# Differential attention of a hybrid diffusion step: scores by half partitions, two sets of score banks, work moved between engines

## The reference

```
def diff_attention(q, k, v, lam):
    # q (B,Lq,H,2,dh), k (B,Lk,H,2,dh), v (B,Lk,H,2dh); blocks of 128 queries
    s = einsum('bqhmd,bkhmd->bhmqk', qblk, k) * dh ** -0.5
    p = softmax(s, axis=-1)
    a = p[:, :, 0] - lam * p[:, :, 1]
    return einsum('bhqk,bkhe->bqhe', a, v)
...
o_d = diff_attention(q_d, k_all, v_all, lam)
o_d = rmsnorm(o_d, diff_subln_g) * (1.0 - lam_init)
branch_d = o_d.reshape(B, L, DIFF_V_W) @ w_diff_out
```

## Time and profile before

| what | value |
|---|---|
| time of the runs | 1432.61, 1429.55, 1432.03 us, median 1432.03 |
| the profiled execution, first to last instruction | 1432.7 us |
| TensorE busy | 1363.0 us, 95% |
| VectorE, ScalarE, GpSimd busy | 638.5, 452.0, 112.9 us |
| attention, from the first scores to the last stored output tile | 651.30 to 796.99 us |

### The profile page before, as it was taken

How to read it: one execution, slowest core, us unless ns; L and a number is a source line. 1 busy time by engine, 2 the same in 40 slices (tenths; PEclk the granted TensorE clock), 3 DMA queues, 4 the chain that set the end, 5 groups by cost and what they waited for, 6 DMA issues and landing times.

```text
span 1432.7 us, 24335 instructions
## 1 busy us (share of the span) xinstructions
PE 1363.0 (95%) x9545; PEld 1291.3 (90%) x9545; DVE 638.5 (45%) x935; ACT 452.0 (32%) x777; POOL 112.9 (8%) x205
## 2 busy tenths in 40 slices
PE   4899999999999999998999899989999999999996
PEld 1699998899999999996777599989999999999996
DVE  3733112466557534645777644352324232333244
ACT  5421313344211122216777522242211122212223
POOL 1011000300111111202111300000000000000000
PEclk9999999999999999999999999999999999999998
DMA  9444231143444343530000014202121212221211
GB/s 303 146 116 118 59 88 44 53 134 116 144 150 137 103 128 101 168 128 30 0 0 0 30 59 147 89 30 88 59 88 61 87 59 88 73 75 61 72 45 73
DMA packets 100820, 127.05 MB, mean 89 GB/s; under 512 B 3433, under 2 KB 91986, under 8 KB 100770
## 3 DMA queue, kind: packets, MB, share of 16 engines
q1 hardware_dynamic: 90624, 95.20, 21.1%
q0 software_dynamic: 8928, 30.09, 6.7%
q10 hardware_dynamic: 1218, 1.07, 0.2%
HBM read 115.34 MB, written 4.72 MB: 84 GB/s over the span
## 4 chain that ended last, share of the span: by engine, by line
PE 88%; DVE 4%; issue 2%; SPq 2%; ACT 2%; POOL 1%; DMA 1%; DVEq 0%; ACTq 0%; POOLq 0%
PE psum L340 49%; PE psum L355 26%; PE psum L760 4%; PE psum L787 2%; PE psum L774 2%; SPq L481 1%; PE psum L321 1%; DVE probs L1359 1%; PE psum L762 1%; PE psum L671 1%; DMA ada_a<-in_w_ada 1%; POOL diag L635 1%; PE psum L388 1%; PE psum L389 1%; PE psum L722 1%
## 5 line engine op out<-in xcount | busy, mean ns | idle before, releaser
L305 DVE TENSOR_TENSOR w_lo<-w_raw,w_hi 128x2048 fp32r<-128x2048 f32 x78 | 178.7, 2291 | 307.8 <-ACT w_hi L300 299.8
L340 PE MATMUL psum<-h_hi,w_lo 128*128 128x320 f32 x1344 | 308.5, 311 | 3.4 <-DVE hf L431 1.4
L340 PE MATMUL psum<-h_hi,w_hi 128*128 128x320 f32 x1344 | 307.4, 310 | 0.0
L340 PE MATMUL psum<-h_lo,w_hi 128*128 128x320 f32 x1344 | 307.2, 310 | 0.0
L340 PEld LDWEIGHTS psum<-h_hi,w_lo 128*128 128x128 f32 x1344 | 225.4, 189 | 4.4 <-issue 4.3
L340 PEld LDWEIGHTS psum<-h_lo,w_hi 128*128 128x128 f32 x1344 | 225.9, 189 | 0.0
L340 PEld LDWEIGHTS psum<-h_hi,w_hi 128*128 128x128 f32 x1344 | 225.7, 189 | 0.0
L300 ACT ACTIVATE w_hi<-w_raw 128x2048 fp32r<-128x2048 f32 x77 | 146.8, 1906 | 149.1 <-PE psum L355 97.7
L355 PE MATMUL psum<-w_lo,h_hi 128*128 128x256 f32 x480 | 136.1, 283 | 0.0
L355 PE MATMUL psum<-w_hi,h_lo 128*128 128x256 f32 x480 | 135.8, 283 | 0.0
L355 PE MATMUL psum<-w_hi,h_hi 128*128 128x256 f32 x480 | 135.8, 283 | 0.0
(11 more groups left out here) (214 smaller groups left out, 1842.6 us busy)
## 6 DMA issues: line engine op xcount, KB each, us to landing
w_raw<-in_w_in SPq DMA_DIRECT2D x32, 1024.0 KB, 5.9
ada_b<-in_w_ada POOLq DMA_DIRECT2D x32, 512.0 KB, 4.1
w_raw<-in_w_ffn_gate SPq DMA_DIRECT2D x11, 1024.0 KB, 5.1
w_raw<-in_w_ffn_up SPq DMA_DIRECT2D x11, 1024.0 KB, 5.1
ada_a<-in_w_ada SPq DMA_DIRECT2D x8, 1024.0 KB, 12.4
w_raw<-in_w_ffn_down SPq DMA_DIRECT2D x8, 1024.0 KB, 5.1
w_raw<-in_w_ret_out SPq DMA_DIRECT2D x4, 1024.0 KB, 5.1
swapped<-qk_d POOLq DMA_DIRECT2D x32, 128.0 KB, 2.5
```

Of the source, the lines that this page charges most:

```text
L305: dve.tensor_tensor(w_lo[s][:, :, :], w_raw[s][:, :, :], w_hi[s][:, :, :].bitcast(F32), ALU.subtract).then_inc(w_lo_done, 1)
L340: last = pe.matmul(bank(4 * par + 2 * j + h, HALF), w[:, k, cs], x[:, k, h * HALF:(h + 1) * HALF], start=(k == 0 and n == 0), stop=(k == K ...
```

## The change

- The scores of map m are computed from the 64 partitions that hold it, for queries and keys alike, by matmuls over 64 partitions. `qz` and its copies and the clearing of `qz` on GpSimd are gone. A latent tile takes five matmuls: keys of 128, 384, 512, 128 and 128, in turn from the lower and the upper half, with a wait (`at_shared`) ahead of the fifth, which shares a bank with the first.
- There are two sets of three score banks (0 to 2 and 3 to 5); tile n uses set n % 2 and waits for the exponentials of tile n - 2. The two maps lie 896 columns apart, so that one maximum instruction (line 1303 of the new kernel) reads both.
- The maps are combined on GpSimd in two instructions, a product in place (line 624) and a sum (line 626).
- The transposes go to banks 6 and 7: four blocks in bank 6, the fifth in the first quarter of bank 7. The outputs go to the third quarter of bank 7, for all tiles. The fifth transpose of tile n therefore waits until the output of tile n - 1 has been read (`at_oe`).
- The output is read by VectorE, not ScalarE: a scaled copy (line 1318) and then a product with a row sum (line 1320) that waits for the copy.
- All 40 tiles are written out with no loop. Slot s holds on TensorE `outputs(s-4)`, `weights_T(s-3)`, `scores(s+1)`; on VectorE `evacuate_o(s-4)`, `factor(s-1)`, `maximum(s+1)`; on ScalarE `evacuate_T(s-3)`, `exp(s)`.

```diff
             def scores(n):
+                if n >= 2:
+                    pe.wait_ge(at_e, 2 * n - 2)
...
+                    pe.matmul(bank(b0 + 1, P), qk_d[m0, h, q], kc_T[m0, h, :], start=True, stop=True).then_inc(at_shared, 1)
+                    pe.matmul(bank(b0 + 2, LAT - P), qk_d[m1, h, q], qk_d[m1, k, P:LAT], start=True, stop=True)
+                    pe.matmul(bank(b0), qk_d[m0, h, q], qk_d[m0, k, 0:LAT], start=True, stop=True)
+                    pe.matmul(bank(b0 + 2, P, LAT - P), qk_d[m1, h, q], kc_T[m1, h, :], start=True, stop=True)
+                    pe.wait_ge(at_shared, n - h + 1)
+                    last = pe.matmul(bank(b0 + 1, P, LAT - P), qk_d[m1, h, q], qk_d[m1, k, 0:P], start=True, stop=True)
...
+            def weights_T(n):
                 pe.wait_ge(at_a, n + 1)
+                if n >= 1:
                     pe.wait_ge(at_aT, n)
+                for c in range(keys_of(n) // P):
+                    if c == LAT_TILES and n >= 1:
+                        pe.wait_ge(at_oe, n)
+                    last = pe.transpose(bank(6 + c // 4, P, (c % 4) * P), probs[:, n % 3, 0, c * P:(c + 1) * P], ident[:, :])
...
+            for slot in range(-1, QT + 4):
+                if 0 <= slot - 4:
+                    outputs(slot - 4)
+                if 0 <= slot - 3 < QT:
+                    weights_T(slot - 3)
+                if slot + 1 < QT:
+                    scores(slot + 1)
...
+            def maximum(n):
+                dve.wait_ge(at_s, n + 1)
+                at_, apart = 3 * (n % 2) * BANK, (896 if n % TILES < LAT_TILES else 2 * BANK)
+                both = psum[:, at_:at_ + 2 * apart].rearrange("p (m k) -> p m k", m=2)[:, :, 0:keys_of(n)]
+                dve.reduce_max(sm[:, n % 8, 0:2], both, axis=AX.X, negate=True).then_inc(at_max, 1)
...
+            def evacuate_o(n):
+                h, t = n // TILES, n % TILES
+                x, r0, out = bank(7, P, 2 * P), sm[:, n % 8, 4:5], o_nat[:, t, h * P:(h + 1) * P]
+                if t == LAT_TILES:
+                    dve.wait_ge(k_stored, 16)
+                dve.wait_ge(at_o, n + 1)
+                dve.tensor_scalar(out, x, r0, None, ALU.mult).then_inc(at_oc, 1)
+                dve.wait_ge(at_oc, n + 1)
+                dve.scalar_tensor_tensor(junk_o[:, :], x, r0, out, ALU.mult, ALU.mult,
+                                         accum_out=stats[:, n:n + 1]).then_inc(at_oe, 1)
...
+            for slot in range(-1, QT + 4):
+                if 0 <= slot - 4:
+                    evacuate_o(slot - 4)
+                if 0 <= slot - 1 < QT:
+                    factor(slot - 1)
+                if slot + 1 < QT:
+                    maximum(slot + 1)
```

More of the change, by code:

```diff
@@ L766, in scores @@
                 last.then_inc(at_s, 1)
-            def weights_T(h0, t0, first=False):
-                h, t, n = tile_of(h0, t0)
+            def weights_T(n):
                 pe.wait_ge(at_a, n + 1)
-                if not first:
+                if n >= 1:
                     pe.wait_ge(at_aT, n)
-                for c in range(TILES if t < LAT_TILES else 1):
-                    last = pe.transpose(bank(4 + c // 4, P, (c % 4) * P), probs[:, PBUF[t], 0, c * P:(c + 1) * P], ident[:, :])
+                for c in range(keys_of(n) // P):
+                    if c == LAT_TILES and n >= 1:
+                        pe.wait_ge(at_oe, n)
+                    last = pe.transpose(bank(6 + c // 4, P, (c % 4) * P), probs[:, n % 3, 0, c * P:(c + 1) * P], ident[:, :])
@@ L815, in _ @@
-            pe.wait_ge(at_oe, 2 + DH * TILES)
+                if n >= 1:
+                    pe.wait_ge(at_oe, n)
+                hs = slice(h * P, (h + 1) * P)
+                chunks = keys_of(n) // P
+                for c in range(chunks):
+                    val = v_d[:, LAT_TILES, hs] if t == LAT_TILES else v_d[:, c, hs] if c < LAT_TILES else v_cache[:, hs]
+                    last = pe.matmul(bank(7, P, 2 * P), aT[:, n % 3, c, :], val, start=(c == 0), stop=(c == chunks - 1))
+                last.then_inc(at_o, 1)
@@ L1075, in _ @@
+            set_table(ACT.Exp)
+            for slot in range(QT + 3):
+                if slot >= 3:
+                    evacuate_T(slot - 3)
+                if slot < QT:
+                    exp(slot)
+                if slot == QT:
+                    set_table(ACT.Sqrt)
             root("normo", DH * TILES)
@@ L1361, in _ @@
-            maximum(0, 0, 0)
-            maximum(0, 0, 1)
-            maximum(0, 1, 0)
-            weights(0, 0, 0)
-            maximum(0, 1, 1)
-            weights(0, 0, 1)
-            maximum(0, 2, 0)
-            weights(0, 1, 0)
-            maximum(0, 2, 1)
-            weights(0, 1, 1)
-            with dve.Fori(0, DH - 1) as h:
-                for t in range(2, TILES + 2):
-                    maximum(h, t + 1, 0)
-                    weights(h, t, 0)
-                    maximum(h, t + 1, 1)
-                    weights(h, t, 1)
@@ L1377, in _ @@
-            for t in range(2, TILES):
-                if t + 1 < TILES:
-                    maximum(DH - 1, t + 1, 0)
-                weights(DH - 1, t, 0)
-                if t + 1 < TILES:
-                    maximum(DH - 1, t + 1, 1)
-                weights(DH - 1, t, 1)
-            dve.wait_ge(at_oe, 2 + DH * TILES)
+            def maximum(n):
[3 more added lines that the diff above has]
+                dve.reduce_max(sm[:, n % 8, 0:2], both, axis=AX.X, negate=True).then_inc(at_max, 1)
```

184 lines of the change are left out of this document (54 added, 130 removed).

## The result

| | before | changed |
|---|---|---|
| median, us | 1432.03 (5 runs, 1429.08 to 1433.95) | 1443.76 (5 runs, 1440.39 to 1447.4) |
| profiled span, us | 1432.7 | 1442.1 |

The changed kernel takes 1.0067 times as long (95% interval 1.0045 to 1.009): 6 to 13 us more. The forecast was 1439 us, slower.

A forecast was written before the change was run, and what follows sets the result against it. TensorE, all but full in the attention stage, was taken to bound the kernel. Heads of 18.0 us and a longer stage end shift the last transpose by 6.5 us: 1432.7 + 6.5 = 1439.2, stated as 1439, range 1428 to 1464.

The forecast's parts named there:

- The ring of a latent slot: Per latent tile: maximum, output read, signal, fifth transpose, scores, signal, next maximum form one chain of 3.94 us.
- The other slots: Slots of a head around the prompt tile, from maximum 2 to 3, 3 to 4, 4 to 0: 2.9, 2.94, 4.27 us.
- Halves side by side: Latent tile's scores on TensorE: lower and upper array halves overlap in part, 1.2 us from first to last start.
- my two ends: Bounds on a latent tile's scores, first to last start: 2.03 us without overlap, 0.96 with full overlap.
- The drain at each change of row set: Rival: TensorE's array empties twice a slot, 0.34 us per latent slot, 9.5 us in all, 1448 to 1449; chance 0.15.
- my lower end: Latent tile's scores with the array halves fully overlapping: 0.96 us from first to last start.
- my bounds: GpSimd's product when combining the maps: between 0.8 and 1.6 us.
- The clock: Rival: TensorE's clock falls because it idles; a head some 23.5 us, the time about 1478; chance 0.04.
- Both ends: Attention stage: first maximum near 653.9, tile 4's at 663.0; last transpose 11.4 us behind the last maximum, 3.27 a tile.
- The sum: Last transpose at 800.4 against 793.93 us, a shift of 6.5 that goes to the kernel's end: 1439 us.
- the first rival: Array halves do not run side by side in the scores: latent slots 4.77, a head 20.9, 1461 us; chance 0.25.

The follow-up runs named there:

- the control: Kernel before, without the zero-padded GpSimd copies and with TensorE's loop written out, each score matmul over all 128 partitions (output not the reference's): 1429.93 us, ratio 0.9972.
- scores first: Changed kernel with TensorE taking the scores of tile s+1 ahead of the transposes of tile s-3: 1469.32 us, ratio 1.026.
- exponentials first: Changed kernel with scores ahead of transposes on TensorE, and exponentials ahead of the copy of the transposed weights on ScalarE: 1536.32 us, ratio 1.0691.
- one bank set: Changed kernel with all tiles using score banks 0 to 2, a tile's scores waiting for the previous tile's exponentials: 1567.68 us, ratio 1.0921.
- the version with the short end: Kernel with ScalarE's output copy, plus two late sets of transposes in free score banks ahead of outputs and tile 38 combined on VectorE: 1421.28 us, ratio 0.9908.

## Why the prediction was right, step by step

- *The ring of a latent slot.* Right in place, and nearly in size: 3.87 and 3.88 us measured, 3.94 forecast. Term by term: maximum 1.41 (1.42), output read and signal 0.79 (0.90), fifth transpose to scores 0.26 (0.11), scores 1.09 (1.20), signal 0.33 (0.31). The ring was shown by taking one instruction out of it (a slot of 3.48) and by making its scores longer (5.97 us more a head).
- *The other slots.* 2.71 (2.9), 3.00 (2.94) and 4.23 (4.27). A head 17.69 (18.0).
- *Halves side by side.* I chose 1.2 between 0.96 and 2.03; it is 1.09. Undone, with the 0.32 of the added wait taken off, the overlap is worth 1.08 us a tile, the difference of my two ends (1.07).
- *The drain at each change of row set.* I gave it 0.15, with nothing in the rows for it. It exists, at nearly the price that I had put on it, 0.34 to 0.39 us for both changes. In the changed kernel the change to 64 partitions lies in the ring, in two places: 0.15 us more between the fifth transpose and the scores (0.26 against 0.11; 0.05 of it is the slower pace of a first transpose, which the control shows behind a wait too), and 0.10 inside the scores, whose first matmul starts its second pass at 704.55, 0.21 behind the first, where a pace of 0.11 was reckoned. The change back lies beside the maximum. So the ring holds 0.25 us that my sum put at nothing, and the scores without it would be 0.99, near my lower end and not my 1.2. The two errors and the output read, 0.11 shorter than I took it, cancel. This is luck in the size, not in the place.
- *GpSimd.* The product takes 1.88 us, outside my bounds of 0.8 to 1.6. No wait of the quoted slot is for it, because 2 to 3 us were hidden; it became the second limit as soon as the ring was shortened.
- *The clock.* I gave a fall of the clock 0.04 and thought of the whole stage. It fell in part: in two of seven heads, 1.13 us each, so 2.3 of the seven heads' 4.1 us. Without that the heads would have cost 1.8.
- *Both ends.* Tile 4's maximum came 11.70 us behind the first scores (11.85), the last transpose 11.58 behind the last maximum (11.4), 3.34 a tile (3.27). The end of the stage is the largest loss, 7.5 us, more than the heads.
- *The sum.* +6.5 forecast for the stage, +6.25 measured. The difference of the medians is 11.7: 6.25 in the stage, 0.7 behind it, 2.5 before the first scores, most of it the clock there, and 2.3 because the profile of before was of an execution slower than its median. I had taken its span, 1432.7, as standing for a time only 0.7 over the median. So some 7 us can be followed to places that the change reaches, and the low end of the interval, 6.4, is near that. Two slips in the working change little: the first rival's slots add up to 21.0 a head, not 20.9, and its 2.03 rests on 2.14 for the scores where the rows give 2.16.

Where my expectations missed later (three times: scores first, exponentials first, one bank set) the step left out was the same: what stands ahead of an instruction in its own engine's queue, and which buffer's reader it waits for. A fourth miss, the half-array scores in the kernel before, was the drain taken as nothing. In the prediction I had followed the ring over TensorE and VectorE, and had taken ScalarE as never late. That held for the order as it was, and for no other.

## What to carry to other kernels

Shortening an engine's work pays only where that engine is not in a ring with another: here TensorE lost 2.3 us of work a head, and each slot grew to the ring of maximum, output read, transpose and scores, because two uses of one PSUM bank and VectorE's order of work tied them. Look for the instruction that frees the bank and let it do only that: 1443.8 became 1432.3 this way. Putting it on another engine, together with three more edits, gave 1421.4, and there the gain lay in the slots around the prompt tiles. Before moving a step in an in-order queue, write down for every engine what it waits for there, round to the start; and when a stage is run some tiles deeper, price its end, which was the largest single loss here.

## What the runs showed of the hardware

- Two f32 matmuls over 64 partitions each, on the lower and the upper half of the array, start 0.01 us apart and run side by side: a tile's scores need 1.09 us against 2.49 in turn, of which 0.32 are the wait that keeps them in turn.
- Going from 128 to 64 partitions and back costs TensorE 0.34 to 0.39 us at full clock, some 3.8 us over the ten stays of a head; 2.58 of them show against a program with full rows.
- GpSimd's product of 640 f32 elements with one value per partition takes 1.88 us, longer than its sum of two such tensors, 1.54.
- VectorE's combination of two SBUF operands takes 0.885 us in each of the eight tiles of the version with ScalarE's copy, and 2.16 us in the version with the short end, where GpSimd's sum had started 0.05 us before it:

```profile
773.39 1.53 POOL L640 TENSOR_TENSOR probs<-probs 128x640 f32<-128x640 f32 x1
773.44 2.16 DVE L1344 SCALAR_TENSOR_TENSOR probs<-probs,sm 128x640 f32<-128x640 f32 x1
```

  The row sum from SBUF took 0.544 on average where the bank was freed by the copy alone and GpSimd was busy for 14.71 of a head's 16.45 us, and 0.29 at the least. The Trainium skill, "SBUF — State Buffer", Practical consequences, says that a VectorE instruction with two SBUF inputs contends with a GpSimd instruction that reads SBUF; these rows agree.
- VectorE's read of its accumulator takes 0.08 us, ScalarE's 0.20.
- TensorE's granted clock fell to 0.50 for a while in two of seven heads with the same waits, at 1.1 us each; what set these two apart no row shows.
